# Three engines instead of two for the taps of a depthwise convolution: TensorE 3 channel tiles, VectorE 3, GpSimd 2

## The chip, the cores and the metric

The kernel runs on one core of one Trainium2 chip. The metric is the device time in microseconds, as the median of several runs. A core has TensorE (PE in the profile, its weight loads PEld), VectorE (DVE), ScalarE (ACT), GpSimd (POOL) and SyncE (SP), which issues most of the loads. Each engine works off its own queue in program order, and the queues meet only at semaphores.

## The reference

Two blocks follow each other over 256 positions of 1024 channels: a first one (a gated recurrence, a dense feed-forward part, an attention, a mixture of eight experts), and a second one that begins with a Conformer convolution module and goes on with feed-forward parts and an attention. The change is in the convolution module of the second block:

```python
u = hn @ w_pw1 + b_pw1
a, g = jnp.split(u, 2, axis=-1)
u = a * jax.nn.sigmoid(g)
u = lax.conv_general_dilated(u, kern, window_strides=(1,),
        padding=((CONV_WIDTH - 1, 0),), ...,
        feature_group_count=D_MODEL) + b_dw     # CONV_WIDTH = 31, per channel
u = layernorm(u, ln_g, ln_b)
u = jax.nn.silu(u)
return u @ w_pw2 + b_pw2
```

The convolution is causal and per channel: each of the 1024 channels is a sum of 31 shifted copies of itself, each times a weight of its own, plus a bias.

## The kernel before

Weights come from DRAM into a ring of buffers. For each half of a chunk, ScalarE writes a rounded copy (`wh`, L767) and VectorE the rest (`wl`, L1259), and TensorE multiplies three products of the parts. ScalarE and VectorE do this `split` in their program order, between the other work of a stage.

The convolution stage starts with a projection in four chunks of 256 output channels each (`project`, L2269). For each chunk and each block of 128 positions, VectorE adds the bias (L1712), ScalarE takes the sigmoid (L1083), VectorE multiplies (L1718), TensorE transposes (L1909) and ScalarE copies the result to `uT` (L748), which holds the channels in 8 tiles of 128 partitions, each with 256 positions behind 30 zeros. Chunk c yields tiles 2c and 2c+1; the semaphore `s_Te` counts the copies. So tiles 2 and 3 are there after the second chunk.

Then the taps. They are shared between two engines:

- TensorE has tiles 4 to 7 (`CV_PE`). ScalarE writes for each tap a diagonal matrix of the 128 weights (`diag`, L1099, a ring of 16), and TensorE multiplies it with the shifted tile and adds up in PSUM (L2278, 31 taps a tile). After 31 taps ScalarE adds the bias and copies the sum to `cT` (`conv_sum`, L1092). TensorE starts on them when all of `uT` is there. Its fp32 product stands in the trace as two matmuls, so 124 taps are 248 records.
- VectorE has tiles 0 to 3 (`CV_DVE`). The first tap of a tile is L1693 (product and bias), the 30 others are L1695, an in-place product and sum of 128x256 elements. After one tap index of all its tiles it waits for its own last instruction (`link`). The first 12 taps of tiles 0 and 1 are done early, six after chunk 2 and six after chunk 3. Then it signals that the bias rows are free (L1725, `s_rows_free` to 5), waits for all of `uT`, does the rest, and signals `cv_dw`.

TensorE waits for `cv_dw` and for the last `conv_sum`, and transposes `cT` back (L2287) to `ctm`; ScalarE copies it, VectorE computes statistics and normalises (L1210 to L1733), TensorE has meanwhile the residual (L1950), then transposes again (L1866), ScalarE applies SiLU (L1112), and the second projection begins.

GpSimd issues small loads and clears buffers. Its queue around this stage reads, in order: after `s_rows_free` 4, loads of the rows of `conv_b_pw1`; after `s_rows_free` 5 (the signal of L1725), loads of the rows of `conv_b_pw2` and `final_norm` (L644); after the second transposes (`s_T` T_cn + 4), two clears (L657) and a load. Long before, in the routing of the experts (L702 to L719), it does some sixty tiny operations of 1 to 16 elements per partition, each with a wait for the one before (`link`).

Of the kernel before, what the change touches and what calls it, by code (L numbers as in the profile page):

```python
# [33 lines left out]
D = 1024  # L34
SEQ = 256
NB = SEQ // P
KT = D // P
# [8 lines left out]
CONV = 31  # L46
# [13 lines left out]
ALU = mybir.AluOpType  # L60
# [120 lines left out]
def build(nc, t):  # L181
    ctx = ExitStack()
    with ctx:
        _program(nc, t, ctx)


def _program(nc, t, ctx):
    def sb(name, shape, dt=F32):
        return ctx.enter_context(nc.sbuf_tensor(name, shape, dt))

    def sem(name):
        return ctx.enter_context(nc.semaphore(name))
# [23 lines left out]
    arena = sb("arena", [P, 5, 2 * D])  # L216
    vecs = sb("vecs", [P, 10, KT])
    cols, rowcols = vecs[:, 0:7, :], vecs[:, 7:10, :]
    wdw = sb("wdw", [P, KT, CONV])
# [65 lines left out]
    uT = flat(arena[:, 0:2, :])[:, 0:KT * (SEQ + PADC)].rearrange("p (k n) -> p k n", k=KT)  # L285
    cT = as_cm(arena[:, 2, :])
    ctm = as_tm(arena[:, 3, :])

    CV_DVE, CV_PE = range(4), range(4, KT)
    DIAGS = 2 * D // P  # L290
    diag = arena[:, 3, :].rearrange("p (i n) -> p i n", i=DIAGS)
    EARLY = 6
    squares = arena[:, 3, D:2 * D]

    vec_rows = arena[0:10 * KT, 2, D:D + P]
    wdw_rows = arena[0:CONV, 1, 0:D]
# [4 lines left out]
    def level_banks(n):  # L301

        return acc[:, 0:2, :] if n % 2 == 0 else tp[:, :, :]
# [67 lines left out]
    g_cv, t_cv = pl.take_steps([1] * 8)  # L371
# [47 lines left out]
    s_vecs = sem("s_vecs")  # L419
# [11 lines left out]
    s_Te = sem("s_Te")  # L431
# [15 lines left out]
                                      "hi", "lo", "used", "down", "yeh", "yel", "give", "added")}  # L447
    m_ready = [sem(f"moe_ready{r}") for r in range(RAW)]
    cv_dw, cv_n = sem("conv_done"), sem("conv_normed")
    cv_diag, cv_tap, cv_sum = sem("conv_diagonals"), sem("conv_taps"), sem("conv_sums")  # L450
    f_L, f_A, f_D, f_C, f_CT, f_ct = (sem(n) for n in ("f_logits", "f_act", "f_vec", "f_sum", "f_sumT", "f_sumT_sb"))
    s_wh, s_wl = sem("s_wh"), sem("s_wl")
# [23 lines left out]
    n = N_RC + NB  # L476
# [152 lines left out]
    def _(pool):  # L629
# [12 lines left out]
        def load_rows(*srcs):  # L642
            for i, s in enumerate(srcs):
                pool.dma_start(rows[:, i * D:(i + 1) * D], bc(s)).then_inc(s_rows, 16)  # L644

        with nc.allow_non_contiguous_dma(reason="small parameters"):
# [75 lines left out]
            load_rows(t["conv_b_pw1_2"][0][0:D], t["conv_b_pw1_2"][0][D:2 * D])  # L722
            pool.wait_ge(s_rows_free, 5)
            load_rows(t["conv_b_pw2_2"][0], t["final_norm_2"])

            pool.wait_ge(s_T, T_cn + 4)
            clear_halves(2)
# [1123 lines left out]
    def _(pe):  # L1851
# [21 lines left out]
        def split_product(out, x_hi, x_lo, w_hi, w_lo, start, stop):  # L1873

            mm(out, x_hi, w_hi, start=start, stop=False)  # L1875
            mm(out, x_hi, w_lo, start=False, stop=False)  # L1876
            return mm(out, x_lo, w_hi, start=False, stop=stop)  # L1877
# [142 lines left out]
        for n in range(NH * NB + 2):  # L2020
            if n < NH * NB:


                j, b = n // NB, n % NB
# [7 lines left out]
                for q in range(2):  # L2032
                    for part in (lfh, lfl):
                        ins = mm(level_banks(n)[:, q, :], part[:, b, j * P:(j + 1) * P],
                                 lev[b][:, q, :], start=part is lfh, stop=part is lfl)
                ins.then_inc(hg_m, 1)
            if 1 <= n <= NH * NB:

                m = n - 1
                j, b = m // NB, m % NB  # L2040
# [13 lines left out]
            if 2 <= n:  # L2054
                m = n - 2
                j, b = m // NB, m % NB
# [6 lines left out]
                for l in range(8):  # L2063
                    ins = mm(up[:, m % 2, 0:P], hgS[:, l, :], v[:, b, j * P:(j + 1) * P], start=(l == 0 and b == 0),  # L2064
                             stop=(l == 7))
# [67 lines left out]
        for b in range(NB):  # L2133
            ins = nc.tensor.transpose(up[:, 0, b * NE:(b + 1) * NE], few[0:NE, b * P:(b + 1) * P], ident[0:NE, 0:NE])
# [5 lines left out]
        for k in range(KT):  # L2140
            ins = nc.tensor.transpose(tp[:, 1, k * CONV:(k + 1) * CONV], wdw_rows[:, k * P:(k + 1) * P], ident[0:CONV, 0:CONV])
# [130 lines left out]
        for i, k in enumerate(CV_PE):  # L2272
            if i >= 2:
                pe.wait_ge(cv_sum, i - 1)
            for j in range(CONV):
# [2 lines left out]
                mm(up[:, k % 2, 0:SEQ], diag[:, x % DIAGS, :], uT[:, k, j:j + SEQ], start=(j == 0),  # L2278
                   stop=(j == CONV - 1)).then_inc(cv_tap, 1)
        pe.wait_ge(cv_dw, 1)  # L2280
        pe.wait_ge(cv_sum, len(CV_PE))
        for b in range(NB):
            for q in range(2):
                tt = T_cback + 2 * b + q
                turn_bank(tt)
                for k in range(4):
                    ins = nc.tensor.transpose(tp[:, tt % 2, k * P:(k + 1) * P], cT[:, 4 * q + k, b * P:(b + 1) * P], ident)  # L2287
# [5 lines left out]
        for i, d in enumerate(after):  # L2293
            if i == 1:
# [20 lines left out]
                for b in range(NB):  # L2315
                    ins = nc.tensor.transpose(tp[0:NH2, 0, b * P:(b + 1) * P], fx[:, 5, b, :], ident)
# [38 lines left out]
            for k in range(2):  # L2355
                for b in range(NB):
                    ins = nc.tensor.transpose(tp[:, d["T_p"] % 2, (2 * k + b) * P:(2 * k + b + 1) * P],
                                              pe_tm[:, b, k * P:(k + 1) * P], ident)
# [5 lines left out]
            for s in range(4):  # L2364
                c, b = s // NB, s % NB
                for k in range(2):
                    ins = split_product(acc[:, s, :], pe_Th[:, k, b * P:(b + 1) * P], pe_Tl[:, k, b * P:(b + 1) * P],
                                        w[0][:, k, c * W:(c + 1) * W], w[1][:, k, c * W:(c + 1) * W], k == 0, k == 1)
# [34 lines left out]
```

## Time and profile before

| | us |
|---|---|
| median of 3 runs | 2592.39 (2592.31 to 2593.82) |
| the profiled execution | 2589.41 |
| its span in the trace | 2587.3 |

Busy over the span: TensorE 2405.0 us (93%), its weight loads 1981.4, VectorE 1806.5 (70%), ScalarE 1463.2 (57%), GpSimd 53.3 (2%). The line L2278 of the convolution taps has 56.5 us of TensorE. The chain that ended last is 80% TensorE, 9% VectorE, 5% ScalarE and 4% DMA.

Times in the rows below are microseconds from the start of the span, unless marked ns. A row of a timeline is: start, length, engine, line, operation, output<-inputs, shapes, count, and in brackets the idle time before it and what ended it. Neighbours of one kind are merged into one row with a count. A name such as `arena` covers several of the program's views: `uT`, `cT` and `diag` all lie in `arena`.

### The profile page before, as it was taken

To read this page: it belongs to the slowest core of one execution; us is meant where nothing else is said; L and a number is where in the kernel's file an instruction comes from. 1 tells how busy PE (TensorE), PEld (TensorE's weight loads), DVE (VectorE), ACT (ScalarE), POOL (GpSimd) and SP (SyncE) were. 2 spreads that over 40 slices of the span, in tenths; PEclk is the share of its full clock that TensorE was granted. 3 is DMA by queue.
4 is the path that set the end of the run, shared out by engine and by line. 5 is a ranking of instruction groups with operands and counts; after the bars stand their busy time and mean duration, and the time that the engine had idled before them with its cause. 6 is when DMAs were issued, how large, how long until landed. Compare 5 with 4: busy or idle time off the path is not lost.

```text
span 2587.3 us, 29857 instructions
## 1 busy us (share of the span) xinstructions
PE 2405.0 (93%) x11253; PEld 1981.4 (77%) x11253; DVE 1806.5 (70%) x1720; ACT 1463.2 (57%) x1550; POOL 53.3 (2%) x97
## 2 busy tenths in 40 slices
PE   7888999877999999999999999996979998999997
PEld 6676887756888888888888888875768876777885
DVE  5675545774889898889888898986845455544454
ACT  4622434353677777777767676764754345445444
POOL 0000000002100000000000000000000000000000
PEclk9999999998999999999999999997989998999998
DMA  7203555405999999999999999976214553403541
GB/s 293 98 4 114 180 195 192 166 1 188 362 334 379 337 375 343 368 347 368 347 368 349 357 358 343 373 258 211 82 37 163 192 182 127 151 21 130 195 179 49
DMA packets 264085, 589.67 MB, mean 228 GB/s; under 512 B 8402, under 2 KB 39346, under 8 KB 263729
## 3 DMA queue, kind: packets, MB, share of 16 engines
q1 hardware_dynamic: 261376, 579.38, 61.9%
q0 software_dynamic: 2608, 8.93, 1.1%
q8 instruction: 67, 1.10, 0.2%
q14 instruction: 34, 0.27, 0.0%
HBM read 587.22 MB, written 1.05 MB: 227 GB/s over the span
## 4 chain that ended last, share of the span: by engine, by line
PE 80%; DVE 9%; ACT 5%; DMA 4%; issue 2%; SPq 0%; DVEq 0%; ACTq 0%
PE up L1875 15%; PE up L1877 15%; PE up L1876 15%; PE acc L1875 8%; PE acc L1876 7%; PE acc L1877 7%; DMA raw<-in_ffn_w 3%; DVE wl L1259 3%; ACT wh L767 3%; PE up L2278 2%; PE acc L2158 1%; PE up L2064 1%; PE tp L1866 1%; PE tp L2194 1%; PE acc L2050 1%
## 5 line engine op out<-in xcount | busy, mean ns | idle before, releaser
L1573 DVE TENSOR_TENSOR wl<-raw,wh 128x2048 fp32r<-128x2048 f32 x378 | 864.7, 2291 | 128.4 <-ACT wh L973 126.1
L973 ACT ACTIVATE wh<-raw 128x2048 fp32r<-128x2048 f32 x378 | 727.1, 1924 | 225.2 <-PE up L1877 135.9
L1875 PE MATMUL up<-wh,xTh 128*128 128x512 f32 x1888 | 756.5, 401 | 27.6 <-DVE wl L1259 7.7
L1877 PE MATMUL up<-wh,xTl 128*128 128x512 f32 x1888 | 742.5, 393 | 0.0
L1876 PE MATMUL up<-wl,xTh 128*128 128x512 f32 x1888 | 741.7, 393 | 0.0
L1259 DVE TENSOR_TENSOR wl<-raw,wh 128x2048 fp32r<-128x2048 f32 x171 | 389.2, 2291 | 387.7 <-ACT wh L767 386.9
L767 ACT ACTIVATE wh<-raw 128x2048 fp32r<-128x2048 f32 x171 | 324.4, 1916 | 389.6 <-PE up L1877 218.0
L1875 PEld LDWEIGHTS up<-wh,xTh 128*128 128x128 f32 x1888 | 359.6, 190 | 107.5 <-issue 20.2
L1877 PEld LDWEIGHTS up<-wh,xTl 128*128 128x128 f32 x1888 | 358.3, 190 | 77.5
L1876 PEld LDWEIGHTS up<-wl,xTh 128*128 128x128 f32 x1888 | 359.5, 190 | 71.0
L1875 PE MATMUL acc<-wh,hTh 128*128 128x512 f32 x864 | 339.7, 393 | 7.8 <-DVE wl L1573 4.8
L1876 PE MATMUL acc<-wl,hTh 128*128 128x512 f32 x864 | 338.8, 392 | 0.0
L1877 PE MATMUL acc<-wh,hTl 128*128 128x512 f32 x864 | 338.6, 392 | 0.0
L1875 PEld LDWEIGHTS acc<-wh,hTh 128*128 128x128 f32 x864 | 164.0, 190 | 42.7 <-DVE wl L1573 5.0
L1877 PEld LDWEIGHTS acc<-wh,hTl 128*128 128x128 f32 x864 | 163.8, 190 | 34.5
L1876 PEld LDWEIGHTS acc<-wl,hTh 128*128 128x128 f32 x864 | 163.9, 190 | 34.1
L806 ACT ACTIVATE half<-up 128x512 f32<-128x512 f32 (+1 forms) x78 | 41.9, 538 | 105.5 <-PE up L1877 105.4
L1866 PE MATMUL tp<-cst,arena 128*128 128x128 f32 x176 | 35.7, 356 | 56.2 <-DVE arena L1681 24.1
L983 ACT ACTIVATE hTh<-tp 128x512 fp32r<-128x512 f32 x63 | 37.8, 601 | 82.0 <-PE tp L2194 82.0
L1866 PEld LDWEIGHTS tp<-cst,arena 128*128 128x128 f32 x176 | 25.7, 179 | 67.3 <-DVE arena L1681 25.7
L2278 PE MATMUL up<-arena 128*128 128x256 f32 x248 | 56.5, 392 | 1.6 <-ACT arena L1099 1.6
L2278 PEld LDWEIGHTS up<-arena 128*128 128x128 f32 x248 | 48.8, 197 | 9.3 <-ACT arena L748 1.9
(341 smaller groups left out, 1961.0 us busy)
## 6 DMA issues: line engine op xcount, KB each, us to landing
raw<-in_moe_w_gate SPq DMA_DIRECT2D x126, 1024.0 KB, 6.8
raw<-in_moe_w_up SPq DMA_DIRECT2D x126, 1024.0 KB, 7.1
raw<-in_moe_w_down SPq DMA_DIRECT2D x126, 1024.0 KB, 6.1
raw<-in_ffn_w SPq DMA_DIRECT2D x32, 2048.0 KB, 8.8
raw<-in_hg_w_in SPq DMA_DIRECT2D x7, 2048.0 KB, 13.2
raw<-in_da_w_in SPq DMA_DIRECT2D x6, 2048.0 KB, 8.2
raw<-in_ffn_w_gate SPq DMA_DIRECT2D x11, 1024.0 KB, 6.6
raw<-in_ffn_w_up SPq DMA_DIRECT2D x11, 1024.0 KB, 10.9
```

Of the source, the lines that this page charges most:

```text
L767: f(wh[:, q % SPLITS, :], raw_half(q), ACT.Copy).then_inc(s_hi, 1)
L806: f(out, in_, func, **kw).then_inc(s_act, 1)
L973: f(wh[:, x % SPLITS, :], raw[:, x % RAW, :], ACT.Copy).then_inc(moe["hi"], 1)
L983: f(hTh[:, 0, :], tp[:, 0, :], ACT.Copy).then_inc(moe["Th"], 1)
L1259: V.tensor_tensor(wl[:, q % SPLITS, :], raw_half(q), wh[:, q % SPLITS, :].bitcast(F32), ALU.subtract).then_inc(s_lo, 1)
L1573: V.tensor_tensor(wl[:, x % SPLITS, :], raw[:, x % RAW, :], wh[:, x % SPLITS, :].bitcast(F32), ALU.subtract).then_inc(moe["lo"], 1)
L1866: ins = nc.tensor.transpose(tp[:, tt % 2, k * P:(k + 1) * P], src[:, b, (4 * q + k) * P:(4 * q + k + 1) * P], ident)
L1875: mm(out, x_hi, w_hi, start=start, stop=False)
L1876: mm(out, x_hi, w_lo, start=False, stop=False)
L1877: return mm(out, x_lo, w_hi, start=False, stop=stop)
L2050: mm(acc[:, 2 + l // 4, (l % 4) * P:(l % 4 + 1) * P], B[:, first + l, :], A[:, first + l, :], start=True, stop=True)
L2278: mm(up[:, k % 2, 0:SEQ], diag[:, x % DIAGS, :], uT[:, k, j:j + SEQ], start=(j == 0), stop=(j == CONV - 1)).then_inc(cv_tap, 1)
```

## The change

Tiles 5, 6 and 7 stay with TensorE, tiles 0, 1 and 4 are VectorE's, tiles 2 and 3 GpSimd's. TensorE's loop over `CV_PE` runs over 93 taps instead of 124, and ScalarE writes 93 diagonals. VectorE's tiles are still three in number for the tap indices from 12 on, and one (tile 4) for the indices before that.

GpSimd has no combined product and sum here. For each tap index it issues two products of 128x256 elements into a buffer of two slots (`cv_products`, in a part of `arena` that is free then), and one sum of 128x512 elements in place onto both tiles of `cT`. The first tap writes `cT` itself, with the bias. The sum waits for the two products in front of it and for the sum before. That is 62 products and 30 sums. The block stands in GpSimd's queue behind the two row loads that wait for `s_rows_free` 5. TensorE has one more wait, for the 30 sums, ahead of the transposes back.

```diff
@@ -286,11 +286,12 @@
     cT = as_cm(arena[:, 2, :])
     ctm = as_tm(arena[:, 3, :])
 
-    CV_DVE, CV_PE = range(4), range(4, KT)
+    CV_DVE, CV_POOL, CV_PE = [0, 1, 4], [2, 3], [5, 6, 7]
     DIAGS = 2 * D // P
     diag = arena[:, 3, :].rearrange("p (i n) -> p i n", i=DIAGS)
     EARLY = 6
     squares = arena[:, 3, D:2 * D]
+    cv_products = arena[:, 4, 0:D].rearrange("p (a i n) -> p a i n", a=2, i=2)
 
     vec_rows = arena[0:10 * KT, 2, D:D + P]
     wdw_rows = arena[0:CONV, 1, 0:D]
@@ -447,6 +448,7 @@
                                       "hi", "lo", "used", "down", "yeh", "yel", "give", "added")}
     m_ready = [sem(f"moe_ready{r}") for r in range(RAW)]
     cv_dw, cv_n = sem("conv_done"), sem("conv_normed")
+    cv_pool, cv_product = sem("conv_pool_sums"), sem("conv_pool_products")
     cv_diag, cv_tap, cv_sum = sem("conv_diagonals"), sem("conv_taps"), sem("conv_sums")
     f_L, f_A, f_D, f_C, f_CT, f_ct = (sem(n) for n in ("f_logits", "f_act", "f_vec", "f_sum", "f_sumT", "f_sumT_sb"))
     s_wh, s_wl = sem("s_wh"), sem("s_wl")
@@ -722,6 +724,25 @@
             load_rows(t["conv_b_pw1_2"][0][0:D], t["conv_b_pw1_2"][0][D:2 * D])
             pool.wait_ge(s_rows_free, 5)
             load_rows(t["conv_b_pw2_2"][0], t["final_norm_2"])
+
+            pool.wait_ge(s_vecs, 2)
+            pool.wait_ge(s_Te, t_cv[3] + 1)
+            sums = cT[:, CV_POOL[0]:CV_POOL[0] + 2, :]
+            for j in range(CONV):
+                for i, k in enumerate(CV_POOL):
+                    src = uT[:, k, j:j + SEQ]
+                    if j == 0:
+                        ins = nc.gpsimd.tensor_scalar(cT[:, k, :], src, wdw[:, k, 0:1], rowcols[:, 0, k:k + 1], ALU.mult, ALU.add)
+                    else:
+                        if j > 2:
+                            pool.wait_ge(cv_pool, j - 2)
+                        ins = nc.gpsimd.tensor_scalar(cv_products[:, j % 2, i, :], src, wdw[:, k, j:j + 1], None, ALU.mult)
+                    ins.then_inc(cv_product, 1)
+                if j > 0:
+                    pool.wait_ge(cv_product, 2 * j + 2)
+                    if j > 1:
+                        pool.wait_ge(cv_pool, j - 1)
+                    nc.gpsimd.tensor_tensor(sums, sums, cv_products[:, j % 2, :, :], ALU.add).then_inc(cv_pool, 1)
 
             pool.wait_ge(s_T, T_cn + 4)
             clear_halves(2)
@@ -2278,6 +2299,7 @@
                 mm(up[:, k % 2, 0:SEQ], diag[:, x % DIAGS, :], uT[:, k, j:j + SEQ], start=(j == 0),
                    stop=(j == CONV - 1)).then_inc(cv_tap, 1)
         pe.wait_ge(cv_dw, 1)
+        pe.wait_ge(cv_pool, CONV - 1)
         pe.wait_ge(cv_sum, len(CV_PE))
         for b in range(NB):
             for q in range(2):
```

## Rows read from the trace of the kernel before

**Rows 1.** The chain that ended last: start, length, engine, tile, line; conv stage.
```profile
1834.42 56.55 PE up L2278 x248
...
1891.58 0.65 PE tp L2287 x4
```

**Rows 2.** Busy time by stretch; granted TensorE clock is the column PEclk (1.00 is full).
```profile
core 0: us, PE busy (x) PEld busy (x) DVE busy (x) ACT busy (x) POOL busy (x), PEclk, DMA share, GB/s
...
1834.00:1840.00 6.00, 5.58 (x13) 4.54 (x14) 5.86 (x11) 6.00 (x21) 0.00 (x0) 0.50 0.30 125
1840.00:1888.00 48.00, 48.00 (x224) 41.98 (x224) 43.31 (x103) 41.63 (x107) 1.18 (x2) 1.00 0.07 23
...
1893.80:1897.40 3.60, 3.60 (x12) 1.52 (x11) 2.36 (x7) 2.36 (x4) 0.00 (x0) 1.00 0.00 0
...
1903.40:1906.00 2.60, 1.67 (x7) 1.30 (x8) 0.69 (x1) 2.57 (x7) 0.00 (x0) 0.50 0.00 0
```

**Rows 3.** Timeline of ScalarE: the first two sums of a tile, and the last.
```profile
1851.27 0.47 ACT L1092 ACTIVATE arena<-up,vecs 128x256 f32<-128x256 f32 x1
...
1864.66 0.47 ACT L1092 ACTIVATE arena<-up,vecs 128x256 f32<-128x256 f32 x1
...
1891.00 0.47 ACT L1092 ACTIVATE arena<-up,vecs 128x256 f32<-128x256 f32 x1 [6.51 <-PE up L2278]
```

**Rows 4.** Timeline of VectorE: early taps of two tiles, then the main stretch.
```profile
1822.09 4.55 DVE L1695 SCALAR_TENSOR_TENSOR arena<-arena,wdw 128x256 f32<-128x256 f32 x10
...
1842.06 42.51 DVE L1695 SCALAR_TENSOR_TENSOR arena<-arena,wdw 128x256 f32<-128x256 f32 x98
```

**Rows 5.** Timeline of GpSimd: its row loads during the taps.
```profile
1841.49 0.65 POOL L644 DMA_DIRECT2D big<-in_conv_b_pw  x1 [69.30 <-DVEq L1725]
1842.14 0.53 POOL L644 DMA_DIRECT2D big<-in_final_norm  x1
```

**Rows 6.** GpSimd's costs: groups by line and form, one line's spread (min/median/max), timeline.
```profile
L657 POOL MEMSET raw<- 64x2048 f32 x2 | 3.6, 1805 | 0.1
...
L695 POOL TENSOR_TENSOR rt<-rt 128x8 f32<-128x8 f32 x6 | 1.2, 203 | 0.5
...
L717 POOL TENSOR_TENSOR rt<-gate,ex 128x16 f32<-128x16 f32 x3 | 0.7, 220 | 0.3
...
L662 POOL MEMSET ncT<- 128x256 f32 x1 | 0.3, 331 | 0.0
...
L710 POOL TENSOR_SCALAR ex<-ex x3: 237/251/2155, 630.6 to 645.1; 128x8 f32<-128x8 f32 x3
...
632.32 0.22 POOL L714 TENSOR_TENSOR rt<-rt,ex 128x16 f32<-128x16 f32 x1
632.62 0.48 POOL L695 TENSOR_TENSOR rt<-rt 128x8 f32<-128x8 f32 x2
```

**Rows 7.** Timelines of VectorE and of GpSimd in the routing stage.
```profile
634.22 6.69 DVE L1573 TENSOR_TENSOR wl<-raw,wh 128x2048 fp32r<-128x2048 f32 x3
...
634.07 2.49 POOL L695 TENSOR_TENSOR rt<-rt 128x8 f32<-128x8 f32 x2
636.64 2.12 POOL L696 TENSOR_TENSOR gate<-rt 128x2 f32<-128x2 f32 x1
638.85 2.15 POOL L710 TENSOR_SCALAR ex<-ex 128x8 f32<-128x8 f32 x1
641.08 0.20 POOL L711 TENSOR_TENSOR ex<-ex 128x8 f32<-128x8 f32 x1
```

**Rows 8.** Timelines of TensorE and ScalarE behind the taps.
```profile
1893.88 3.60 PE L1950 MATMUL acc<-h,cst 128*128 128x512 f32 x8
1897.32 1.07 PE L1866 MATMUL tp<-cst,arena 128*128 128x128 f32 x8
...
1905.42 1.12 PE L1866 MATMUL tp<-cst,arena 128*128 128x128 f32 x4 [0.88 <-DVE xTl L1273]
...
1900.41 1.51 ACT L1112 ACTIVATE stage<-tp,vecs 128x128 f32<-128x128 f32 x4
```

## The prediction

> **What bounds the kernel now.** I read the chain that ended last first, over the convolution stage. It runs through TensorE's taps without a break: L2278 from 1834.42 for 56.55 us, to 1890.97, and at 1891.58 the transposes back begin [rows 1]. So in this stage TensorE decides, and the step that releases the next stage is ScalarE's last sum, 1891.00 + 0.47 us [rows 3]. Then I read who else works for that same moment. VectorE's last tap ends at 1842.06 + 42.51 = 1884.57 [rows 4], 7 us ahead of the transposes. GpSimd has nothing to do but two row loads, at 1841.49 and 1842.14 [rows 5]. The stretches show what the clock does: 0.50 granted in the first 6 us of the taps, after an idle TensorE, and 1.00 from 1840 to 1888 [rows 2]. At full clock a tile of 31 taps takes 1864.66 - 1851.27 = 13.39 us [rows 3].
>
> The end of the stage is thus the latest of three, TensorE, VectorE and, with the change, GpSimd. I work out each and take the latest.
>
> **TensorE.** It loses one tile of 31 taps. The slow start of the clock stays, because it comes from the idle time in front, so the tile that goes costs 13.39 us. The taps end at 1890.97 - 13.39 = 1877.6, and with the sum of 0.47 us TensorE's share is ready at 1878.1. ScalarE has 31 diagonals less and stays ahead as before. This saving, 13.4 us, is the most that the change can bring, and it counts only if the two others are done by 1878.1.
>
> **VectorE.** Before, 98 taps took 42.51 us, 0.434 us each [rows 4]. The 24 early taps stay as they are. After the signal of L1725, at about 1841.3 (GpSimd's load that it releases starts at 1841.49 [rows 5]), 69 taps are left instead of 100: 12 of tile 4 alone, each with a wait for the last, and 19 times 3. With a wait for every second tap the early ones took 4.55 / 10 = 0.455 us [rows 4]; with one for each I take 0.50. That is 12 x 0.50 + 57 x 0.434 = 30.7 us, so 1872, if nothing disturbs it. VectorE would no longer be near the end.
>
> **GpSimd, when it starts.** The block needs tiles 2 and 3, and these are there after the second chunk. But a queue runs in order, and the block stands behind the row loads that wait for `s_rows_free` 5. In the trace this wait ends at 1841.49, after 69.30 us, by L1725, and the two loads are issued by 1842.14 + 0.53 = 1842.7 [rows 5]. L1725 is not moved by the change. So GpSimd starts at 1842.7 and not in the second quarter: the head start that the change names isn't there. Until 1891.5 it has 48.8 us for 31 tap indices, 1.57 us each (1.6 with the first sum missing); to gain all of TensorE's saving it has 35.4 us, 1.14 us each.
>
> **GpSimd, what a tap index costs.** No row shows its operations at this size; I bound them.
> - The sum, two inputs, 512 elements. From 8 to 16 elements the time goes from 203 to 220 ns [rows 6], 2.1 ns an element; 220 + 496 x 2.1 gives 1.27 us. The lower bound is the rate at which it clears memory, (1805 - 331) / 1792 = 0.82 ns an element [rows 6]: 331 + 256 x 0.82 = 0.54 us. I take 1.27, since the row is of the same operation.
> - A product, one input, 256 elements. Below: 0.33 us, a clear of the same size, which reads nothing. Above: 251 ns at 8 elements plus 248 x 2.1, 0.78 us [rows 6]. It reads one operand and not two, so I take the middle, 0.55.
> - The wait of the sum for its products: the small operations start 0.30 us apart where one lasts 0.22 [rows 6], so 0.08 us.
>
> A tap index costs 2 x 0.55 + 1.27 + 0.08 = 2.45 us; the bounds are 1.28 and 2.91. Thirty-one of them less the first sum are 31 x 2.45 - 1.35 = 74.6 us: undisturbed, GpSimd ends at 1842.7 + 74.6 = 1917.3. (At the bounds: 1881.8 and 1931.6.) This alone is 26 us behind the present end.
>
> The Trainium skill (GPSIMD Engine Reference, Engine selection) says that an operation with one input is roughly line-rate on GpSimd. No row here shows such a product at this size. By that rule a product would take an estimated 0.25 + 256 / 1.2 GHz = 0.46 us and the stage would end about 5.6 us sooner, which changes neither sign nor size.
>
> **GpSimd and VectorE beside each other.** In the routing stage VectorE runs three splits of 128x2048 in a row, each with both inputs in SBUF, 6.69 us. GpSimd's operations, 0.20 us elsewhere, take 2.12 and 2.15 us there, and a pair 2.49, each until one of the three is over; at 641.08 the next takes 0.20 again [rows 7]. So an operation of GpSimd that reads SBUF is held while such a VectorE instruction runs, and comes in between two. VectorE lost nothing there, but GpSimd's operations had 1 to 8 elements. A tap of L1695 also has two inputs in SBUF (`uT` and `cT`), and every operation of the new block reads. From 1842.7 on, VectorE has some 66 taps left. They and GpSimd's 92 operations have to pass one after the other as far as they move data: each tap adds between 0 (it has no part in the conflict) and its whole 0.434 us. GpSimd's fixed part, 0.19 us or so (203 ns at 8 elements less 8 x 2.1), can run beside a tap, so I take 0.434 - 0.19 = 0.24 us, 66 x 0.24 = 16 us; the bounds are 0 and 28.6. It does not matter which of the two ends last; they share the sum. GpSimd's and VectorE's shares are ready at 1917.3 + 16 = 1933.3.
>
> The Trainium skill (SBUF — State Buffer, Who interferes with whom) calls this an exclusive lock of a port pair for the whole instruction, the other side blocking fully, and names VectorE instructions with two SBUF inputs against GpSimd instructions that read. Rows 7 agree on GpSimd's side. By its wording nothing would overlap, and the taps would cost the whole 28.6 us; that is a rival below.
>
> **The wait on TensorE.** Behind the new wait stand the 16 transposes back, the residual and the second transposes; everything after hangs on them. TensorE is idle from 1877.6 to 1933, and its clock falls as it does now after shorter idle times: 0.50 granted in 1903.4 to 1906, against 1.00 in 1893.8 to 1897.4 [rows 2]. Four transposes take 1.12 us at the low clock; eight take 1.07 at full [rows 8]. The residual, 3.60 us now [rows 8], can take up to twice that. It ends today at the moment at which the second transposes may start (1897.32), and ScalarE needs these at 1900.41 [rows 8], so some 2 us of it are hidden. With transposes about 2.3 us longer and a residual 1 to 3.6 us longer I put 2 us on the path, between 0 and 4. GpSimd's later work (two clears, a load) moves along with its release; nobody waits for it soon.
>
> **The sum.** 1933.3 - 1891.6 = 41.7 us, and 2 us of clock: 43.7. Against the profiled execution of 2589.4 that makes 2633.1. The median is 3.0 us above the profiled one, so I predict 2636.
>
> **The rivals.**
> - *No hold at the taps* (17%): only the plain two-input operation holds GpSimd, not L1695. For it: no row shows the two together. Against it: the same two reads. End 1917.3, +27.7 us, 2620. VectorE's taps would keep their 0.434 us.
> - *Hold for the whole instruction* (25%): 28.6 instead of 16 us, end 1945.9, +56.3 us, 2649. Then the taps and GpSimd's operations never overlap and VectorE ends near GpSimd.
> - *The block starts at the second quarter after all* (4%), at about 1812.7, when both copies of chunk 2 are through. It would be held by four splits and 24 early taps more, some 15 us, delay the projection by a part of that, and end near 1812.7 + 74.6 + 16 + 15 = 1918, 2621. The queue order excludes it as far as I can read.
> - *The other side, faster* (4%): GpSimd computes at the rate at which it clears memory, 1.28 us a tap index, unheld, and ends at 1881.8. Then 1891.5 - 1881.8 gives 9.7 us, 2583. It turns at 1.6 us a tap index, holds included. Against it stands the slope of its own two-input operations, with which the sum alone takes 1.27.
> - *A draw* (5%): 1.5 to 1.75 us a tap index.
>
> **How the numbers follow.** The forecast has 45%, the rivals 17, 25, 4, 4 and 5%. With products of 0.33 us and no hold the end is 1842.7 + 31 x 2.01 - 1.35 = 1903.7, 2605 to 2607; with products of 0.78 and the full hold it is 1960, 2665. The range 2606 to 2662 leaves out the faster case, the draw and the outermost tip. A measurement of this kernel can tell about 0.2%, 5.2 us, from no change. Slower by more: 91%; within: 5%; faster: 4%.
>
> **What would show it.** In the profile of the changed kernel: GpSimd's first product near 1842.7, behind the two row loads; sums of about 1.3 us and products of about 0.55 where VectorE is idle, longer beside its taps; L1695 spaced wider than 0.434 us while GpSimd works; L2278 with 186 records that end near 1877.6; then TensorE idle for some 55 us, in a wait that GpSimd's last sum ends; a low clock in the transposes back. If GpSimd starts near 1812, if a tap index takes under 1.6 us, or if TensorE's wait is ended by ScalarE's sum, the prediction is wrong.

## The result: 2.1% slower, with TensorE waiting for GpSimd

| | median, us | ratio to before, 95% interval |
|---|---|---|
| before | 2592.35 | |
| changed | 2647.68 (2645.37 to 2649.09) | 1.0208 (1.0195 to 1.0221) |

The profiled execution of the changed kernel took 2645.37 us, with a span of 2643.5, against 2587.3 before.

The chain of the changed kernel now has "POOL 3%" in it, where before it had no GpSimd at all. Three views say who decides: the chain's shares of the span by engine, its pieces at the end of the taps (start, length, engine, tile, line), and the waits of the stretch 1840 to 1960 (who waited for whom: us in total, times, longest):

```profile
PE 75%; DVE 9%; ACT 5%; DMA 4%; POOL 3%; issue 3%; SPq 0%; DVEq 0%; ACTq 0%
...
1943.96 1.27 POOL arena L745
1945.32 3.76 PE tp L2309 x16
...
PE tp L2309 <- POOL arena L745: 65.9, 1, 65.9
```

TensorE stands for 65.9 us in front of the transposes back, and what ends this wait is GpSimd's last sum. The engines' timelines, each with its own share of the taps (L2299 TensorE, L1716 VectorE, L735 first products, L739 products, L745 sums):

```profile
1836.23 43.16 PE L2299 MATMUL up<-arena 128*128 128x256 f32 x186 [1.57 <-ACT arena L1120]
1945.32 3.74 PE L2309 MATMUL tp<-cst,arena 128*128 128x128 f32 x16 [65.93 <-POOL arena L745]
...
1823.90 4.55 DVE L1716 SCALAR_TENSOR_TENSOR arena<-arena,wdw 128x256 f32<-128x256 f32 x10
...
1843.55 48.36 DVE L1716 SCALAR_TENSOR_TENSOR arena<-arena,wdw 128x256 f32<-128x256 f32 x68
...
1843.30 0.53 POOL L646 DMA_DIRECT2D big<-in_conv_b_pw  x1 [69.30 <-DVEq L1746]
1843.82 0.53 POOL L646 DMA_DIRECT2D big<-in_final_norm  x1
1844.40 1.45 POOL L735 TENSOR_SCALAR arena<-arena,wdw,vecs 128x256 f32<-128x256 f32 x2
...
1862.15 1.39 POOL L745 TENSOR_TENSOR arena<-arena 128x512 f32<-128x512 f32 x1
1863.53 2.23 POOL L739 TENSOR_SCALAR arena<-arena,wdw 128x256 f32<-128x256 f32 x2
1865.84 1.27 POOL L745 TENSOR_TENSOR arena<-arena 128x512 f32<-128x512 f32 x1
...
1942.06 1.82 POOL L739 TENSOR_SCALAR arena<-arena,wdw 128x256 f32<-128x256 f32 x2
1943.96 1.26 POOL L745 TENSOR_TENSOR arena<-arena 128x512 f32<-128x512 f32 x1
```

The early taps of VectorE start at 1823.90, 1.81 us later than in [rows 4]; so much had passed before the stage, and I take it off in all comparisons. GpSimd starts directly behind its row loads (1844.40), not in the second quarter. TensorE's 186 records end at 1836.23 + 43.16 = 1879.39. VectorE's 68 taps take 48.36 us, 0.711 each, against 0.434 in [rows 4], and end at 1891.91. GpSimd goes on alone for 53 us: a tap index takes 3.14 us at the end (1.82 + 0.08 + 1.24, from one pair of products to the next), and up to 3.7 beside VectorE's taps. Its last sum ends at 1945.22.

Where the 55 us went: ScalarE's first SiLU is at 1955.44 and was at 1900.41 [rows 8], 55.0 us later. Of these, 1.8 lie ahead of the stage, 51.9 up to the transposes back (1945.32 - 1.81 against 1891.58 in [rows 1]), and 1.3 behind them, where the transposes back run at the clock that fell while TensorE waited:

```profile
1880.00:1940.00 60.00, 0.00 (x0) 0.00 (x0) 11.73 (x16) 0.00 (x0) 58.49 (x57) 0.52 0.00 0
1940.00:1950.00 10.00, 4.68 (x18) 3.82 (x19) 1.65 (x4) 2.67 (x5) 5.06 (x5) 0.50 0.01 2
...
1955.44 1.50 ACT L1133 ACTIVATE stage<-tp,vecs 128x128 f32<-128x128 f32 x4
```

(First two: busy time by stretch, columns as in [rows 2]; the third is ScalarE's timeline.)

### The profile page after: what moved, and what is told of

Its sections match the earlier page's. It is cut to its first block, busy times and chain, and to the rows that moved or that the text cites. A ratio compares the mean times of both kernels' runs of the same rounds, so it can differ in the third digit from the quotient of the medians.

```text
span 2643.5 us, 29791 instructions
## 1 busy us (share of the span) xinstructions
PE 2397.3 (91%) x11191; PEld 1975.5 (75%) x11191; DVE 1812.1 (69%) x1689; ACT 1450.4 (55%) x1518; POOL 151.5 (6%) x189
## 4 chain that ended last, share of the span: by engine, by line
PE 75%; DVE 9%; ACT 5%; DMA 4%; POOL 3%; issue 3%; SPq 0%; DVEq 0%; ACTq 0%
PE up L1896 15%; PE up L1898 15%; PE up L1897 15%; PE acc L1896 7%; PE acc L1897 7%; PE acc L1898 7%; DMA raw<-in_ffn_w 4%; DVE wl L1280 3%; ACT wh L788 3%; POOL arena L745 1%; PE acc L2179 1%; POOL arena L739 1%; PE tp L1887 1%; PE up L2085 1%; PE tp L2215 1%
## 5 line engine op out<-in xcount | busy, mean ns | idle before, releaser
L1887 PEld LDWEIGHTS tp<-cst,arena 128*128 128x128 f32 x176 | 26.3, 182 | 65.9 <-DVE arena L1702 25.7
L2309 PE MATMUL tp<-cst,arena 128*128 128x128 f32 x16 | 3.7, 427 | 65.9 <-POOL arena L745 65.9
```

## The experiments

All are versions of the changed kernel or of the kernel before, compared with runs of the kernel before on the same chip. The median of these was 2592.7 us beside e1 to e4, 2595.4 beside e5, 2593.9 beside e6 to e9 and 2596.9 beside e10, so a difference of a few us between rows of different chips means little. e1, e5 and e10 are single executions, e2 and e7 two; what they show is read from their traces. e1, e2, e5 and e10 leave out a part of the taps.

| run | us | what it is |
|---|---|---|
| e2_no_vector_taps | 2641.3 | changed, VectorE's late taps left out |
| e1_sums_out | 2598.9 | changed, GpSimd's sums left out |
| e10_products_waiting | 2609.3 | as e1, a wait before each product |
| e5_forms | 2592.2 | eleven forms of GpSimd operations in place of its taps, VectorE's late taps left out |
| e3_early | 2628.5, ratio 1.0139 (1.0122 to 1.0156) | block ahead of the row loads |
| e4_one_product | 2626.5, ratio 1.0129 (1.0112 to 1.0146) | one product of 512 elements |
| e7_early_one_product | 2622.3, ratio 1.0115 (1.0097 to 1.0134) | both |
| e6_no_gpsimd | 2601.1, ratio 1.0033 (1.0020 to 1.0046) | TensorE 3 tiles, VectorE 5 |
| e8_seven_taps | 2593.1, ratio 0.9998 (0.9989 to 1.0007) | before, 7 taps moved to VectorE |
| e9_projection_only | 2593.6, ratio 1.0002 (0.9993 to 1.0011) | before, GpSimd only in the projection |

**How much GpSimd loses to VectorE's taps.**

```diff
-        for j in range(CONV):
-            tap(j, CV_DVE[2:] if j < 2 * EARLY else CV_DVE)
+        tap(0, CV_DVE[2:])
```

> All of VectorE's taps behind the signal for the bias rows are left out but the first of tile 4 (its three tiles are wrong); GpSimd works alone. What GpSimd loses to VectorE's taps is then seen. By the changed kernel's trace: a tap index takes 3.14 us throughout instead of 3.4 to 3.7 in the first 13, GpSimd's last sum ends 5 us sooner, the time is 2642 us or so (5 to 6 less). By the prediction's term the loss was 16 us, so 2632; by the rival of a hold for the whole instruction 28.6, so 2619.

GpSimd's timeline in this run, first and last:

```profile
1846.56 1.09 POOL L735 TENSOR_SCALAR arena<-arena,wdw,vecs 128x256 f32<-128x256 f32 x2
1847.64 1.82 POOL L739 TENSOR_SCALAR arena<-arena,wdw 128x256 f32<-128x256 f32 x2
...
1940.77 1.26 POOL L745 TENSOR_TENSOR arena<-arena 128x512 f32<-128x512 f32 x1
```

From the first product to the end of the last sum: 1942.03 - 1846.56 = 95.5 us, against 1945.22 - 1844.40 = 100.8 in the changed kernel. So GpSimd loses 5.3 us to VectorE's taps. The time, 2641.3, is 6.4 us less, near what the changed kernel's own trace had led me to expect, and not the 16 of the prediction's term. (The two executions are 4.3 us apart, so the 5.3 of the trace is the better figure.)

**What VectorE loses to which operation.**

```diff
-                    nc.gpsimd.tensor_tensor(sums, sums, cv_products[:, j % 2, :, :], ALU.add).then_inc(cv_pool, 1)
...
-        pe.wait_ge(cv_pool, CONV - 1)
+        pe.wait_ge(cv_product, 2 * CONV)
```

> GpSimd's 30 sums are left out (its two tiles are wrong); the 62 products stay beside VectorE's taps. Theory A, from the changed kernel's trace (a tap of VectorE lasts 1.38 to 1.49 us beside a sum, 0.47 to 0.70 beside a product): only an operation of GpSimd that reads two inputs shuts VectorE out for its whole length. Then VectorE's 68 taps take some 36 us (0.53 each) instead of 48.4, a pair of products stays at 2.0 to 2.2 us beside taps, GpSimd ends near 1844 + 60 = 1904 and the time is about 2607 us. Theory B, every operation of GpSimd that reads shuts VectorE out as long as it runs: 0.7 us a tap or more remain, since GpSimd is as busy as before.

Theory A fell. With the sums gone and only products left, VectorE is slower than with the sums. Its timeline and the spread (min/median/max ns) of L1711, the taps, in this run:

```profile
1841.38 57.99 DVE L1711 SCALAR_TENSOR_TENSOR arena<-arena,wdw 128x256 f32<-128x256 f32 x68
...
L1711 DVE SCALAR_TENSOR_TENSOR arena<-arena,wdw x90: 470/866/979, 1821.7 to 1898.9; 128x256 f32<-128x256 f32 x90
...
1843.68 54.15 POOL L739 TENSOR_SCALAR arena<-arena,wdw 128x256 f32<-128x256 f32 x60
```

57.99 / 68 = 0.853 us a tap, with products 54.15 / 60 = 0.903 us apart: about one tap passes for each product, and GpSimd loses nothing. Theory B fits this run, but not the changed kernel: there five taps pass for three operations (0.711 us a tap, 3.5 us a tap index). One thing that differs is a wait, so I put one in (against e1_sums_out):

```diff
-                        if j > 2:
-                            pool.wait_ge(cv_product, 2 * (j - 1))
+                        pool.wait_ge(cv_product, 2 * j + i)
```

> As in the run without sums (GpSimd's 30 sums are left out, its two tiles are wrong), but each product waits for the one before, which leaves a gap of some 0.08 us between them. There, products back to back let just one tap of VectorE through each (58.0 us for 68 taps, 0.85 each); in the changed kernel, where a wait stands before each sum, two taps passed beside a product. Theory D: what lets a second tap through is the gap, in which VectorE's next tap gets its reads in first. Then VectorE's 68 taps take about 68 / 2 x 0.99 = 34 us, products 0.99 us apart or a little more, and VectorE ends before GpSimd. Theory E: the share is one tap per operation whatever the gaps; then VectorE's taps stay at 0.85 to 1.0 us each and take 58 to 67 us.

```profile
1844.94 36.71 DVE L1710 SCALAR_TENSOR_TENSOR arena<-arena,wdw 128x256 f32<-128x256 f32 x68
...
1847.35 62.59 POOL L738 TENSOR_SCALAR arena<-arena,wdw 128x256 f32<-128x256 f32 x60
```

(VectorE's and GpSimd's timeline.) The same taps and the same products, now 62.59 / 60 = 1.04 us apart: VectorE needs 36.71 us instead of 57.99, 0.54 a tap, two for each product. The forecast of theory D (34 us) is met and that of theory E (58 to 67) is not: waits that leave gaps of some 0.09 us in GpSimd's queue give VectorE 21 us back, for 8.4 us of GpSimd's time. The reason that theory D gives is not shown, though. In the changed kernel the second product of a pair has no gap in front of it, and two taps pass beside it all the same (GpSimd's timeline, then VectorE's in three narrow windows):

```profile
1856.54 2.10 POOL L739 TENSOR_SCALAR arena<-arena,wdw 128x256 f32<-128x256 f32 x2
1858.72 1.27 POOL L745 TENSOR_TENSOR arena<-arena 128x512 f32<-128x512 f32 x1
...
1856.76 1.09 DVE L1716 SCALAR_TENSOR_TENSOR arena<-arena,wdw 128x256 f32<-128x256 f32 x2
...
1857.88 0.97 DVE L1716 SCALAR_TENSOR_TENSOR arena<-arena,wdw 128x256 f32<-128x256 f32 x2
...
1858.78 1.49 DVE L1716 SCALAR_TENSOR_TENSOR arena<-arena,wdw 128x256 f32<-128x256 f32 x1
```

So one wait in three operations is enough there. What is shown is the effect of the waits. A rival that no run separates from the gap is the rhythm: in e1_sums_out nearly all taps begin within 0.14 us of the start of a product, one after the other, and a wait may do no more than break this step. (The run as a whole is 10.4 us slower than e1. About 7 of these lie in this stage, where GpSimd now ends last; 3.5 had passed before it.)

**What a product costs.** The block is replaced by four each of eleven forms, each waiting for the one before, nothing of VectorE beside them; some of them:

```diff
+                lambda: nc.gpsimd.tensor_scalar(p2, u2, w1, None, ALU.mult),
+                lambda: nc.gpsimd.tensor_scalar(p2, u2, 0.5, None, ALU.mult),
+                lambda: nc.gpsimd.tensor_copy(p2, u2),
+                lambda: nc.gpsimd.tensor_tensor(p2, u2, w2_, ALU.mult),
```

> GpSimd's taps are replaced by four each of eleven operations, each waiting for the one before, with VectorE's late taps left out, so that nothing holds them (five tiles are wrong). Measured is what each form costs: products of 128, 256 and 512 elements with a per-partition scalar, with a constant, a copy, a product and an addition of two inputs. If a product costs 0.91 us for 256 elements because its scalar is read from memory once, its slope is that of a copy, 0.8 to 1 ns an element, and the fixed part is large: then 512 elements take about 1.2 us and a constant makes it 0.5. If the slope is what costs (2.6 ns an element), 512 elements take 1.6 us and a constant changes nothing.

Groups by line and form, GpSimd alone (between the bars: busy us, then the mean of one in ns): L740, L738 and L739 are products with a scalar per partition of 512, 256 and 128 elements, L742 and L741 with a constant, L744 and L743 copies, L746 and L745 products of two inputs with repeated weights, L747 and L748 additions. L731 is the first tap of the two tiles, which stands in front of the forms: a product with a scalar and then the sum with a second scalar, the bias.

```profile
L740 POOL TENSOR_SCALAR arena<-arena,wdw 128x512 f32<-128x512 f32 x4 | 6.3, 1563 | 0.4
L742 POOL TENSOR_SCALAR arena<-arena 128x512 f32<-128x512 f32 x4 | 6.0, 1491 | 0.3
L746 POOL TENSOR_TENSOR arena<-arena,wdw 128x512 f32<-128x512 f32 x4 | 4.2, 1038 | 0.3
L738 POOL TENSOR_SCALAR arena<-arena,wdw 128x256 f32<-128x256 f32 x4 | 3.7, 923 | 0.5 <-POOL arena L731 0.2
L741 POOL TENSOR_SCALAR arena<-arena 128x256 f32<-128x256 f32 x4 | 3.4, 850 | 0.3
L747 POOL TENSOR_TENSOR arena<-arena 128x256 f32<-128x256 f32 x4 | 2.6, 638 | 0.3
L744 POOL COPY arena<-arena 128x512 f32<-128x512 f32 x4 | 2.5, 615 | 0.2
L745 POOL TENSOR_TENSOR arena<-arena,wdw 128x256 f32<-128x256 f32 x4 | 2.4, 612 | 0.3
L739 POOL TENSOR_SCALAR arena<-arena,wdw 128x128 f32<-128x128 f32 x4 | 2.4, 604 | 0.4
...
L748 POOL TENSOR_TENSOR arena<-arena 128x128 f32<-128x128 f32 x4 | 1.6, 411 | 0.3
L743 POOL COPY arena<-arena 128x256 f32<-128x256 f32 x4 | 1.6, 402 | 0.2
L731 POOL TENSOR_SCALAR arena<-arena,wdw,vecs 128x256 f32<-128x256 f32 x2 | 1.1, 548 | 0.1
```

The slope is what costs: (1563 - 604) / 384 = 2.5 ns an element for a product with a scalar, against (615 - 402) / 256 = 0.83 for a copy and (1038 - 612) / 256 = 1.66 for a product of two inputs. An addition of two inputs has (638 - 411) / 128 = 1.77. A constant in place of the scalar per partition saves 0.07 us only. So the product that reads one input is slower than the operations that read two (for 256 elements 0.92 us, against 0.61 with repeated weights and 0.64 with two tiles), and one product of 512 elements with two inputs (1.04 us) does the work of two with a scalar (1.85).

It is not the scalar as such that costs. L731 has two scalars and two operations, and takes 0.548 us for the same 256 elements against 0.923 with the product alone; in e2_no_vector_taps its two took 1.09 us and the next two products 1.82. Why is open: L731 also writes to another place and starts at the first position. No run gives all of GpSimd's products this form; by these rows it would save an estimated 60 x 0.375 = 22 us of its share.

**The place in the queue.**

```diff
-            pool.wait_ge(s_rows_free, 5)
-            load_rows(t["conv_b_pw2_2"][0], t["final_norm_2"])
-
             pool.wait_ge(s_vecs, 2)
             pool.wait_ge(s_Te, t_cv[3] + 1)
...
+            pool.wait_ge(s_rows_free, 5)
+            load_rows(t["conv_b_pw2_2"][0], t["final_norm_2"])
```

> GpSimd's block is moved ahead of the row loads that wait for the bias rows, so that it starts when tiles 2 and 3 are ready, near 1814.6 instead of 1844.4. If the place in the queue costs what the prediction says, the taps start 30 us sooner, lose up to 2 us to each of four splits and some more to the early taps, and the time falls by about 20 us, to 2627; still slower than before. Rival: the head start is given back in the projection, since VectorE's splits and additions wait for GpSimd's sums and TensorE waits for them: then under 10 us are gained and TensorE's taps start later than 1836.

It is 19 us faster than the changed kernel, as expected, and still 1.4% slower than before. GpSimd's last sum still decides. GpSimd starts at 1817.10, 29.7 us sooner if the 4.2 us are taken off that this run is late ahead of the stage (a split at 1816.39 against 1812.15 before), and its share takes 1926.82 - 1817.10 = 109.7 us instead of 100.8. A part of the head start is given back in the projection. Timelines of GpSimd, VectorE and TensorE:

```profile
1822.82 3.62 POOL L736 TENSOR_SCALAR arena<-arena,wdw 128x256 f32<-128x256 f32 x2
...
1821.58 1.56 DVE L1739 TENSOR_TENSOR stage<-half 128x256 f32<-128x256 f32 x1 [0.57 <-ACT half L1104]
...
1826.63 7.21 DVE L1716 SCALAR_TENSOR_TENSOR arena<-arena,wdw 128x256 f32<-128x256 f32 x10
...
1842.56 43.08 PE L2299 MATMUL up<-arena 128*128 128x256 f32 x186 [1.38 <-ACT arena L1120]
```

A pair of products that runs into a split takes 3.62 instead of 1.82 us, as in [rows 7]; a small product of VectorE (L1739) 1.56 instead of 0.43; the early taps 7.21 instead of 4.55 in [rows 4]. TensorE's taps start 1842.56 - 4.24 = 1838.3, 3.9 us later than in [rows 1], as the rival said; that costs nothing here, since TensorE then waits 41 us for GpSimd.

**One product in place of two.**

```diff
+                nc.gpsimd.tensor_tensor(cv_products[:, j % 2, :, :], uT[:, CV_POOL[0]:CV_POOL[0] + 2, j:j + SEQ],
+                                        wdw[:, CV_POOL[0]:CV_POOL[0] + 2, j:j + 1].broadcast_to([P, 2, SEQ]), ALU.mult)
```

> The two products of a tap index (128x256 each, a weight per partition as scalar, 0.91 us each) become one product of 128x512 with the weights as a second, repeated input. If a two-input operation of 512 elements takes 1.26 us whatever it computes, a tap index takes 1.26 + 0.08 + 1.26 = 2.6 us instead of 3.14, GpSimd ends 31 x 0.54 = 16.7 us sooner and the time is 2631 us; VectorE, held now by both, ends later than 1892 but not last. Rival: the second input with stride 0 is read more slowly, or the more frequent holds of GpSimd by VectorE's taps eat the gain: then 5 us or less.

It is 21 us faster than the changed kernel, more than the expected 17. But the end has changed hands. VectorE's and GpSimd's timeline:

```profile
1846.23 82.08 DVE L1712 SCALAR_TENSOR_TENSOR arena<-arena,wdw 128x256 f32<-128x256 f32 x68
...
1924.61 1.32 POOL L741 TENSOR_TENSOR arena<-arena 128x512 f32<-128x512 f32 x1
```

GpSimd ends at 1925.93, VectorE at 1928.31. Its 68 taps take 1.207 us each, about one for each of GpSimd's operations: 52.6 us more than the 29.5 they would take undisturbed (68 x 0.434). That VectorE would not be last was wrong.

**Both mends together** (the edits of e3_early and of e4_one_product).

> Both mends together: the block ahead of the row loads and one product per tap index. Theory C, from the two runs before: while GpSimd computes, VectorE gets one tap through for each of its two-input operations (82.1 us for 68 taps, 1.2 us each), so what GpSimd gains VectorE pays, and the two mends don't add up. VectorE's 93 taps start at 1826; until GpSimd ends near 1905 it does some 60, the rest at 0.434 us take it to about 1920: 2618 us, with VectorE ending last. If the gains add up (23 and 18 us), the time is 2605 and GpSimd ends last.

The gains don't add up (19 and 21 us alone, 25 together). GpSimd ends at 1903.66 already, and VectorE's last 68 taps run from 1871.42 for 51.28 us, to 1922.70. A part is paid in the projection already: TensorE's taps begin at 1853.10, 12.9 us later than in [rows 1] if the 5.8 us are taken off that this run is late ahead of the block. Theory C holds (2618 expected, 2622 measured); what GpSimd gains, VectorE pays.

**The same share without GpSimd.**

```diff
-    CV_DVE, CV_PE = range(4), range(4, KT)
+    CV_DVE, CV_PE = range(5), range(5, KT)
```

> The same share for TensorE (tiles 5 to 7), but GpSimd has none: VectorE has tiles 0 to 4. What GpSimd's share was worth is then the difference to the changed kernel. VectorE has 131 taps behind 1841.3, at 0.434 us undisturbed: it ends at 1898, 6.6 us behind the transposes of the kernel before, and the time is about 2600 us. So VectorE alone would do GpSimd's two tiles and be 47 us faster than the changed kernel. If not (2640 or more), VectorE's taps have a cost that I don't see and GpSimd is not what makes the change slow.

```profile
1844.30 54.38 DVE L1695 SCALAR_TENSOR_TENSOR arena<-arena,wdw 128x256 f32<-128x256 f32 x128
...
1898.80 3.78 PE L2287 MATMUL tp<-cst,arena 128*128 128x128 f32 x16 [19.32 <-DVEq L1729]
```

(VectorE's and TensorE's timeline.) 54.38 / 128 = 0.425 us a tap, and 2601.1 us: 47 us faster than with GpSimd, 0.3% slower than before. TensorE waits 19.32 us for VectorE here, against 65.93 for GpSimd in the changed kernel.

**A finer balance, and GpSimd in the projection alone.** Both start from the kernel before.

```diff
+        for j in range(MOVED):
+            tap(j, [KT - 1])
+        dve.wait_ge(cv_tap, len(PE_TAPS))
+        link(V.tensor_tensor(cT[:, KT - 1, :], up[:, (KT - 1) % 2, 0:SEQ], cT[:, KT - 1, :], ALU.add))
```

> The kernel before with a balance by taps instead of tiles and no GpSimd: VectorE does the first 7 taps of tile 7 too, TensorE the other 24, and VectorE adds TensorE's sum from PSUM at the end in place of ScalarE. TensorE's taps end 7 x 0.43 = 3.0 us sooner, VectorE's at 1884.6 + 7 x 0.48 = 1888, just in time: 3 us less, 2589.5 us, 0.1% and so hardly to be told from the kernel before. Rival: each of the seven taps waits for the one before (0.5 us) and the last addition stands behind them, so nothing is gained.

VectorE ends the stage, its addition standing behind the seven taps (1889.60 + 3.09, then 0.42 us from 1892.72). The chain has the transposes back directly behind it:

```profile
1893.26 0.67 PE tp L2293 x4
```

TensorE's taps begin at 1838.96 in this trace, 4.54 us later than in [rows 1], the transposes only 1.68 us later. So the stage itself is 2.9 us shorter, near the expected 3.0, in this one execution. The time doesn't show it: the medians are 0.7 us apart, and the interval runs from 2.9 us faster to 1.8 slower.

```diff
-    EARLY = 6
+    EARLY = 10
...
+            pool.wait_ge(s_Te, t_cv[1] + 1)
...
+            for j in range(1, EARLY):
...
+                nc.gpsimd.tensor_tensor(cT[:, 0:2, :], cT[:, 0:2, :], cv_products[:, j % 2, :, :], ALU.add).then_inc(cv_pool, 1)
...
-                    for j in range(EARLY * (c - 2), EARLY * (c - 1)):
-                        tap(j, CV_DVE[0:2])
```

> The kernel before (TensorE tiles 4 to 7, VectorE 0 to 3), but GpSimd does the first 10 taps of tiles 0 and 1, from chunk 1 of the projection on (about 1802 to 1830), when VectorE has few operations with two inputs in SBUF, and VectorE's 24 early taps fall away there. These stand in the chain that leads to TensorE's first tap with 5.3 us; GpSimd's sums delay a split or a product of VectorE by up to 1.2 us each, 1 to 4 us in all on that chain. TensorE's taps begin 1.5 to 4 us sooner, and the time is 2588 to 2591 us. If GpSimd beside VectorE is a loss even there, TensorE begins later than before and the time is above 2592.

No difference either (within 0.1%). Expected were taps of TensorE that begin 1.5 to 4 us sooner. Ahead of GpSimd's block this run is 5.05 us late (a split at 1805.45 against 1800.40), and the taps begin at 1840.68 against 1834.42, so 1.2 us later than before: GpSimd beside VectorE is a small loss even there. GpSimd does 20 taps and VectorE's 24 early ones fall away, yet a split beside it takes 3.35 us instead of 2.29 and a product of VectorE 1.39 instead of 0.43:

```profile
1830.68 3.35 DVE L1275 TENSOR_TENSOR wl<-raw,wh 128x2048 fp32r<-128x2048 f32 x1 [2.32 <-ACT wh L783]
...
1835.17 1.38 DVE L1734 TENSOR_TENSOR stage<-half 128x256 f32<-128x256 f32 x1 [0.54 <-ACT half L1099]
...
1837.69 1.39 DVE L1734 TENSOR_TENSOR stage<-half 128x256 f32<-128x256 f32 x1 [0.54 <-ACT half L1099]
```

None of the versions that do the whole work is measurably faster than the kernel before.

## Why the prediction was right, and by which steps

- **The bound.** Right, and the core of it: three ends, and the latest decides. TensorE's taps end at 1879.39 - 1.81 = 1877.6, as worked out. Its 13.4 us were saved and are not seen in the time, since TensorE then waits 65.9 us.
- **The start of GpSimd.** Right. The first product starts at 1844.40 - 1.81 = 1842.6 (1842.7 in the sum). e3_early shows that the place in the queue costs 19 us.
- **The sum of 512 elements.** The number is right, 1.26 us against 1.27, but with some luck. It came from the slope between operations of 8 and 16 elements, 2.1 ns an element; additions of 128 and 256 elements have 1.77 in e5_forms, which would give 0.638 + 256 x 0.00177 = 1.09 us for 512. The sum in place takes 0.17 us more than that; which part of its form costs this was not tested.
- **The product.** This term was mis-sized: 0.55 us taken, 0.92 measured, above even the upper bound of 0.78. The step that failed is "It reads one operand and not two, so I take the middle". The time does not follow the operands that are read; e5_forms has 2.5 ns an element for a product with a scalar and 1.66 for one of two inputs. The rows had a hint: at 8 elements the operation with one input took 251 ns and that with two 203 [rows 6]. 0.55 us is, by chance, what the first products with their bias took. The undisturbed share took 95.5 us instead of 74.6, 21 us more. The rule of the Trainium skill (GPSIMD Engine Reference, Engine selection) that one input goes at roughly line-rate fits the copy, 0.83 ns an element, and is three times too fast for the plain product with a scalar.
- **The hold beside VectorE.** The mechanism is there, but this term was mis-sized in the other direction, and its side was wrong: GpSimd lost 5.3 us and not 16, while VectorE lost 48.4 - 29.5 = 18.9. The prediction added the hold to the sum of both engines and said that it does not matter who ends last. It does matter: GpSimd was last by 53 us, and only its own loss lies on the path.
- **The two errors together.** + 20.9 and - 10.7 us give the 10 us by which the transposes back came later than predicted (1943.5 against 1933.3). The total of 2636 was near the measured 2648 partly because the two have opposite signs, and that is luck.
- **The rule of the exclusive lock** (the Trainium skill, SBUF — State Buffer, Who interferes with whom). Where GpSimd's operation has two inputs, the trace agrees for VectorE: about one tap passes for each in e4_one_product. GpSimd is not held for the whole tap there: a tap index takes it 2.59 us in that trace, against an estimated 1.04 + 0.08 + 1.24 = 2.36 alone, so two taps cost it 0.23 us and not 0.87. Beside products with a scalar it does not hold in full: in e10_products_waiting two taps pass for each product, 0.54 us a tap with a product every 1.04 us. The rival built on it (2649) came nearest to the measured time, but not by its reason: it wanted 28.6 us of hold and GpSimd lost 5.3.
- **The clock.** 2 us taken; 1.3 measured up to the SiLU. The transposes back ran at 0.50.

## What to carry to other kernels

Before a share of work goes to GpSimd, read its queue from the stage backwards: the waits in front of the new block decide when it starts, whatever the data allow. Price each form of its operations by a row of the same form and a like size; a form that reads less need not be faster, and one with two operations can be faster than one with a single one (0.55 against 0.92 us). And count what it takes from VectorE: here GpSimd did 28 taps in the 48 us in which both worked (14 tap indices of two tiles, worth 12.2 us of VectorE's time) and cost VectorE 18.9 us, so the help was a loss even before GpSimd ended late.

## What the runs showed of the hardware that I had not expected

- On GpSimd a product with one scalar takes 1.563 us for 128x512 elements in fp32, one of a tile and repeated weights 1.038, a copy 0.615. For 128x256 elements a product with a scalar takes 0.923 us, and a product with a scalar plus a second scalar 0.548.
- With nothing but products back to back, GpSimd let about one tap of VectorE pass for each (0.853 us a tap); with a wait before each product, a gap of some 0.09 us, two passed (0.54 us). The waits cost GpSimd 8.4 us in 60 products and saved VectorE 21. With one wait in three operations two passed beside each product as well.
